# Packing the sparse steps of a product-key expert stage into all but the last six dense beats

## The reference, cut to what matters

```python
def chunk(args):
    xb, ib, gb = args                       # tokens, chosen experts, their gates
    act = jax.nn.gelu(jnp.einsum('td,tkd->tk', xb, u[ib]))
    return jnp.einsum('tk,tkd->td', gb * act, v[ib])
```

## Time and profile before

| | us |
|---|---|
| median of three runs | 3880.43 |
| lowest, highest | 3870.20, 3882.09 |
| the profiled execution | 3892.06 |
| its span, first to last instruction | 3890.4 |
| TensorE busy (PE) | 3244.4 (83%) |
| VectorE busy (DVE) | 2461.6 (63%) |
| ScalarE busy (ACT) | 852.0 (22%) |
| GpSimd busy (POOL) | 895.0 (23%) |
| HBM read, written | 904.52 MB, 35.65 MB |

### The profile page before, as it was taken

One profiled execution on the slowest core, in us unless ns is written; L12 is line 12 of the kernel. 1 busy time (PEld: TensorE's weight loads), 2 busy tenths in 40 slices (PEclk: granted clock), 3 DMA queues, 4 the chain that ended last, 5 costly groups with the idle time before them and its releaser, 6 DMA issues. The chain is left out here.

```text
span 3890.4 us, 39693 instructions
## 1 busy us (share of the span) xinstructions
PE 3244.4 (83%) x13220; PEld 2271.2 (58%) x13220; DVE 2461.6 (63%) x5162; ACT 852.0 (22%) x1940; POOL 895.0 (23%) x856
## 2 busy tenths in 40 slices
PE   6937777877799999999678478777777999999995
PEld 5725566765466666666266255666654666666662
DVE  3573553887686666666646634548866866666666
ACT  2331223127500000000033313221365000000000
POOL 0011201216522222222100122012255222222221
PEclk9968878989899999999889788788888999999997
DMA  3100112169999999999831001121699999999997
GB/s 102 54 0 1 48 33 76 63 219 321 328 393 417 417 417 414 409 415 401 319 97 38 1 1 48 44 77 65 232 317 359 386 416 417 417 416 416 415 403 288
DMA packets 235344, 943.33 MB, mean 242 GB/s; under 512 B 19584, under 2 KB 85632, under 8 KB 164864
## 3 DMA queue, kind: packets, MB, share of 16 engines
q0 software_dynamic: 73728, 536.90, 34.1%
q1 hardware_dynamic: 95360, 370.31, 25.0%
q10 hardware_dynamic: 66048, 33.56, 3.0%
HBM read 904.52 MB, written 35.65 MB: 242 GB/s over the span
## 5 line engine op out<-in xcount | busy, mean ns | idle before, releaser
L1881 PE MATMUL bank<-peer_x_late,xT 128*128 128x256 f32 x4096 | 941.7, 384 | 93.6 <-ACT peer_acts_u L1947 49.9
L1881 PEld LDWEIGHTS bank<-peer_x_late,xT 128*128 128x128 f32 x4096 | 788.7, 193 | 305.8 <-issue 153.0
L2009 DVE CUSTOM_DVE_ANT_0 peer_slots<-peer_slots,wide 128x1024 f32<-128x1024 f32 x512 | 627.8, 1227 | 516.5 <-DMA peer_slots<-in_peer_uv,peer_rows 514.9
L1829 POOL DMA_INDIRECT peer_slots<-in_peer_uv,peer_rows x512 | 534.6, 1044 | 1444.7 <-DVE h L2020 1295.2
L1901 PE MATMUL bank<-ring,peer_acts_u 128*128 128x512 f32 x1280 | 584.8, 601 | 38.4 <-DVE peer_acts_u L2040 29.7
L2020 DVE SCALAR_TENSOR_TENSOR h<-peer_slots,peer_coef,h 128x1024 f32<-128x1024 f32 x416 | 533.7, 1283 | 7.6
L1901 PEld LDWEIGHTS bank<-ring,peer_acts_u 128*128 128x128 f32 x1280 | 245.8, 193 | 294.8 <-issue 283.9
L1901 PE MATMUL bank<-ring,wide 128*128 128x512 f32 x768 | 347.1, 597 | 8.5 <-DMA ring<-in_peer_uv 8.4
L1901 PEld LDWEIGHTS bank<-ring,wide 128*128 128x128 f32 x768 | 146.7, 191 | 161.7 <-issue 146.5
L1870 PE MATMUL bank<-peer_hot 128*128 128x128 f32 x1024 | 154.8, 301 | 77.7 <-ACT peer_hot L1954 77.4
L1870 PEld LDWEIGHTS bank<-peer_hot 128*128 128x128 f32 x1024 | 142.1, 210 | 132.2 <-ACT peer_hot L1954 117.0
(11 more groups left out here) (459 smaller groups left out, 4206.3 us busy)
## 6 DMA issues: line engine op xcount, KB each, us to landing
xT<-in_peer_ut SPq DMA_DIRECT2D x256, 512.0 KB, 16.5
ring<-in_peer_uv SPq DMA_DIRECT2D x256, 512.0 KB, 16.1
gates<-peer_staging ACTq DMA_DIRECT2D x32, 1024.0 KB, 16.0
peer_staging<-gates SPq DMA_DIRECT2D x32, 1024.0 KB, 17.9
ring<-in_w_in SPq DMA_DIRECT2D x48, 512.0 KB, 3.6
ring<-in_peer_wq SPq DMA_DIRECT2D x32, 512.0 KB, 3.6
nsa_w<-in_cmp_w SPq DMA_DIRECT2D x2, 4096.0 KB, 12.1
ring<-in_w_out SPq DMA_DIRECT2D x16, 512.0 KB, 4.3
```

The costliest lines, as they stand in the source:

```text
L1829: nc.gpsimd.indirect_dma_start(out=p.slots[:, n % ROW_SLOTS, :], out_offset=None, in_=A["peer_uv"], in_offset=bass.IndirectOffsetOnAxis(ap ...
L1881: last = nc.tensor.matmul(k.bank[bank_of[j]][:, 0:DENSE], u_raw[:, j % U_RING, b * P:(b + 1) * P], p.x_late[:, b, :], start=b == 0, stop=b ...
L2009: nc.vector.tensor_tensor_reduce(out=u, in0=u, in1=k.wide[:, t, :], scale=1.0, scalar=0.0, op0=ALU.mult, op1=ALU.add, accum_out=p.dots[:, ...
```

## The change

One constant is new, and the last line of `steps_until` divides the steps that are left at beat 82 over 122 beats in place of 128:

```diff
@@
 BEATS = TILES_AT + TILES
+ALONE = 6
@@
     first += 4
-    return first + (min(beat, BEATS) - TILES_AT) * (STEPS - first) // TILES
+    return first + (min(beat, BEATS - ALONE) - TILES_AT) * (STEPS - first) // (TILES - ALONE)
```

## The result

| | before | after |
|---|---|---|
| median of 14 runs each, us | 3884.72 | 3898.14 |
| ratio of the times, 95% interval | | 1.0038 (1.0021 to 1.0055) |
| the profiled execution, us | 3892.06 | 3899.63 |
| its span, us | 3890.4 | 3897.9 |

The account below looks back on a forecast made before the run. DMA and TensorE were taken as full mid-stage, with each layer ending on gathers and rows. Per layer -4.3 + 12.6 + 1.7 = +10.0 us, +20 for two, gives 3912 profiled or 3900 on the median; range 3876 to 3918.

Parts of the forecast that it names:

- What ends a layer: End of each layer before the change: it ends on gathers and rows, 13.5 us after TensorE is through.
- The tail: Behind the last dot, five value tiles put the final additions 20.4 us later in place of 7.8: 12.6 us more per layer.
- the clock term: TensorE's slower clock after the gap before tile 123: 1.7 us per layer taken, 0 and 3.0 kept for the range.
- Beats 82 to 185: Middle of the dense stage: gathers keep their pace, TensorE is not held back, the five-tile lead is gone by 3742 us; cost nothing.
- The last 23 steps at 3.5 us: Steps 233 to 255, value tiles held to the beat: 80.5 us in place of 84.8, 4.3 us saved per layer.
- The last dot: Start of the last sparse dot on VectorE: 4.3 us earlier per layer, near 3856.5 us.
- three signs of being wrong: Last 23 steps below 3.1 us, TensorE still several tiles behind at 3742, or earlier steps changing pace with the table.
- Rival A: Last 23 steps run near VectorE's own pace, 2.87 us each, break-even 3.07; a layer gains 4.5 us, 3871; chance 0.13.
- Rival B: No change to speak of: last steps byte-bound at 3.34 us, no clock ramp; +5 to +9 us, 3885 to 3889; chance 0.20.
- rival D: Last 23 steps stay at 3.69 us: +14.3 us per layer, 3909; counted inside the forecast's 0.62.
- Rival C: Gaps keep TensorE at the lower clock, five tail tiles cost 6.8 us each: 17 more per layer, 3930; chance 0.05.

Follow-up runs that it names:

- the control with early gates: The kernel before, its table unchanged, with VectorE gating two tiles a beat from beat 196 on; ratio 1.0006 (0.9989 to 1.0022) to the kernel before.
- ALONE = 2: The changed kernel with only the constant for beats standing alone set to 2 in place of 6; ratio 0.9993 (0.9980 to 1.0007) to the kernel before.

## Why the prediction was right, and where it was not

- *What ends a layer.* Right. Before, the last dot and 7.8 us; the control with early gates confirms that TensorE could end 10 us sooner for nothing.
- *The tail.* Right in mechanism and size. 20.4 us and 1.7 for the clock were forecast behind the last dot; 22.1 and 20.4 were measured. The five tiles took 19.10 us in layer 0 (row below) and 17.40 in layer 1, behind almost the same idle time (2.16 and 2.11 us), so the clock term was 1.7 in one layer and 0 in the other. The granted clock was 0.66 from 1922 to 1927 us, a mean of the two levels, 1.2 and 2.4 GHz, and 1.00, all at 2.4, from 3858 to 3876. Predicted 14.3 us more than before, measured 14.3 and 12.6.
- *Beats 82 to 185: "I let the gathers keep their pace", and the lead is gone at 3742 us.* Wrong. The pace went from 4.36 to 4.13 us a step and TensorE fell back by three tiles, so the lead stood at five tiles. The waits of L2017 in the trace of before (26.8 us from 3400 to 3730) were not read. They say that in that stretch the pace was not the gathers' own: VectorE was held to a lead over TensorE through ScalarE's order. In the changed kernel VectorE came to that limit later (11.5 us of waits). The last 23 steps started 15.7 and 16.2 us earlier behind the first gate product than before, where the forecast had no gain.
- *The last 23 steps at 3.5 us.* Wrong: 4.17 and 3.96. The value tiles were not held to the beat, since the lead was still there; they were rushed as before, and the pace beside them was that of the rushed stretch of before. The upper end that was named, 4.0, is what came. Beside the 3.68 and 3.76 of before this lost 6.5 and 9.3 us of the gain, where the forecast had 4.3 us of saving in this stretch.
- *The last dot.* These two errors have opposite signs, and it is luck that they came near to cancelling: 4.3 us earlier was forecast, 9.2 and 6.8 came. So the sum, forecast at +10.0 us a layer, measured +5.0 and +5.7 in the profiled executions, and +7.4 by the ratio of all runs. The term that was mis-sized is the last dot, by 2.5 to 4.9 us a layer.
- *Its own signs.* Two of the three signs of being wrong came true: TensorE was five tiles behind at that place, and the steps before it changed pace with the table. The total was right by the tail, not by the account of the middle.
- *Rival A* (the gathers get free) had no part: the slowest part, the last 23 steps, ran at 3.96 and 4.17 us where 3.07 was its break-even. *Rival B* (a byte-bound 3.34) and *rival D* (the pace stays at 3.69) fell too: the pace got slower than either. *Rival C* (slow clock) had one slow start in one layer, not five slow tiles.

Layer 0 of the changed kernel, the five tiles behind the last dot:

```profile
1922.38 19.10 PE L1902 MATMUL bank<-ring,peer_acts_u 128*128 128x512 f32 x40 [2.16 <-DVE peer_acts_u L2041]
```

The page "TensorE: Matmul & The Clock Gate" of the Trainium skill, in its part on the clock gate, calls the ramp under 1% of a typical span. Here it cost 1.7 us of 866 on the path in layer 0 and nothing in layer 1, so for the whole the trace agrees. With ALONE = 2 the slow tile of layer 1 cost 0.5 us at most, since the row additions would have ended the layer 7.8 us behind the last dot in any case and it ended at 8.3.

The 358 GB/s in the specifications of "DMA: Bandwidth & Descriptors" of the Trainium skill is no limit for this one core: 416 GB/s again in the changed kernel from 3500 to 3600 us. The same page, under its measurements, gives about 358 GB/s for each of two cores that both stream; no run here has a second core.

```profile
3500.00:3600.00 100.00, 96.36 (x330) 61.62 (x329) 64.56 (x98) 6.47 (x26) 22.36 (x24) 1.00 1.02 416
```

## What to carry to other kernels

When one stream of work is pulled ahead so that another can stand alone at the end, count what the second still owes from the moment at which it is released, not from its share of beats: here five tiles of 3.43 us, of which 7.8 us of row additions hide only a part. Look at what releases them (here the place of the gate products in VectorE's order); moving that gave back the whole loss, within the noise. And before taking a pace as a resource's own, list every wait of the engine that keeps it, the short ones too: here 16 waits of at most 3.7 us were the mark of a lead that was held.

## What was not expected of the hardware

A fourth gather in flight raised the landing time of each from 9.3 to 12.2 us and did not quicken the last steps of the changed kernel (4.06 to 3.99 us). In the stretch just after the `peer_ut` loads end, DMA moved only 374 GB/s in place of 416, and still the gathers were no faster (4.17 us a step over the last 23 steps of layer 1). The busy share of the DMA engines was 0.96 there against 1.02, so they moved fewer bytes for nearly the same busy time; why is open:

```profile
3796.00:3816.00 20.00, 20.00 (x47) 8.55 (x45) 12.49 (x19) 0.55 (x4) 4.69 (x5) 1.00 0.96 374
```
